# Attention on one Trainium2 core: the meta columns of two query tiles turned in one transpose

## Chip, core and metric

The kernel runs on one core of one Trainium2 chip. The metric is device time in microseconds (us) of one execution, from several executions of the same program. All matrices are float32; matmul operands are kept as a high part (rounded to the matmul's format) and a low part (the rest), so that one product becomes two or three matmuls.

## What is computed

A trunk of two layers on 2048 tokens of width 1024, with 16 learned meta tokens in front. Layer 0 is latent attention with 16 heads; layer 1 is a gated short convolution. Only the attention is touched here. Cut from the reference:

```python
key_chunk = concatenate([zeros(N_META), frame_chunk])      # N_META = 16, chunks of 64 tokens
def attend(qn, qr, q_chunk):
    s = (einsum('bqhd,bkhd->bhqk', qn, k_nope) + einsum('bqhr,bkr->bhqk', qr, k_rope)) * scale
    s = where(key_chunk[None, :] <= q_chunk[:, None], s, NEG_INF)
    p = softmax(s, axis=-1)
    return einsum('bhqk,bkhd->bqhd', p, v)
```

Every query sees the 16 meta keys and all keys up to the end of its own chunk of 64.

## The kernel before

The program has three stages, one after the other. `stage_p` makes keys, queries, values and gates (0 to 559 us of the trace). `stage_b` is the attention (to about 1564 us). `stage_cde` is the output product, the norms and the convolution layer.

**Units, tiles, chunks.** In `stage_b` each of 16 heads has 8 units (L825). A unit u is a pair of query tiles of 128 tokens, the even tile 2u and the odd tile 2u+1; unit 0 has also the tile of the 16 meta queries (`META_TILE`). The keys of a unit are cut into chunks x of 2 to 4 blocks of 128 keys; chunk 0 has the block of the 16 meta keys in front (`blocks_of`, L844). The even tile doesn't see the unit's last block (`tile_blocks`, L850).

**The steps.** Each engine works through a list of steps, written out by hand as a string of letters for one head (L829 to L840) and repeated for all heads, with lags (L841) that let scores run ahead of transposes (9 steps) and transposes ahead of products (6).
- S, TensorE (L1181 to L1191): the scores of one tile and chunk, three matmuls into one of 5 PSUM banks (`split_matmul`, L43 to L45).
- M, VectorE (L1251 to L1273): masks the last 64 keys of the diagonal block (memset, L1265) and takes the row maximum (L1267, L1272).
- E, ScalarE (L1145 to L1161): the exponential, from PSUM to one of 14 slots `p` of 512 columns in SBUF, and the row sums.
- T, TensorE (L1192 to L1209): turns the tile's chunk, one transpose for each block of keys, into `tb` (two buffers in PSUM). The data are the weights and the identity is what moves. The meta block is a transpose with 16 columns of weights. T number n waits for the exponential (L1202) and for the L step n-2 (L1204).
- H, ScalarE (L1162 to L1172): the high part of what was turned, from PSUM to `b_pt_hi`, all blocks of the chunk in one instruction.
- L, VectorE (L1274 to L1282): the low part, PSUM minus high part, to `b_pt_lo`.
- P, TensorE (L1210 to L1230): values times turned probabilities of both tiles of a unit, one matmul for each block over 256 columns (the last block of a unit has 128, the meta block of unit 0 has 272), first with the high part (L1224), then with the low part (L1228), added up in one bank `ob`. The weights are `b_v`, 128 rows by 128 columns (high and low part of the head's values); the meta block's weights have 16 rows of values, and rows of zeros under them (L1089).
- C and A: ScalarE and VectorE (L1288) take the unit's result out of `ob`.

**Beside them.** GpSimd (POOL, L1098 to L1139) splits the next head's keys, queries and values, and pieces of the output weights, into high and low parts, and multiplies earlier heads' results with their gates. SP issues all loads and stores of the stage. The identity has an SBUF tensor of its own (L2207), is loaded once near the end of `stage_p` (L345) and is used by the transposes of `stage_b` (L1207) and of `stage_cde` (L1856).

Of the kernel before, what the change touches and what calls it, by code (L numbers as in the profile page):

```python
# [6 lines left out]
F32 = mybir.dt.float32  # L7
# [6 lines left out]
P = 128  # L14
# [778 lines left out]
def own_memory(nc, ctx, outer, ident, ground, big_hi, big_lo):  # L793
# [8 lines left out]
    o_b, o_t = (arena[:, at:at + 2 * P + META] for at in (T + (NT + 1) * VH, T + (NT + 1) * VH + 2 * P + META))  # L802
    p = arena[:, sum(sizes) - PSLOTS * HALF:].rearrange("p (a b) -> p a b", b=HALF)
# [52 lines left out]

def unit_tiles(u):
    return ([META_TILE] if u == 0 else []) + [2 * u, 2 * u + 1]
# [22 lines left out]
LAST_TURNED = [max(k for k, (_, gg) in enumerate(TURNED) if gg == g) for g in range(len(PRODUCTS))]  # L881
UNIT_ENDS = [g for g, (h, u, x) in enumerate(PRODUCTS) if x == len(UNIT_CHUNKS[u]) - 1]
# [34 lines left out]
def stage_b(nc, own, dram):  # L917
# [6 lines left out]
    with ExitStack() as ctx:  # L924
        sb = lambda n, s, d=F32: ctx.enter_context(nc.sbuf_tensor(n, s, d))
        sem = lambda n: ctx.enter_context(nc.semaphore(n))
        v = sb("b_v", [P, 2, NT + 1, 2 * VH], F32R)
        pt_hi, pt_lo = sb("b_pt_hi", [P, 2, 8 * P], F32R), sb("b_pt_lo", [P, 2, 8 * P], F32R)
# [10 lines left out]
        first_hi, first_split, hi_done = sem("b_first_hi"), sem("b_first_split"), sem("b_hi_done")  # L939
        keys_loaded = lambda h: 64 * (h - 1) + 16  # L940
# [134 lines left out]
        def _(pool):  # L1075
# [66 lines left out]
        def _(act):  # L1142
            act.wait_ge(sums_set, 4)
            for letter, n in SCALAR_STEPS:
                if letter == "E":  # L1145
# [13 lines left out]
                    nc.scalar.activation(p[0:rows, n % PSLOTS, 0:w], banks[0:rows, n % RING, 0:w], ACT.Exp,  # L1159
                                         bias=nmax[0:rows, tile % 8:tile % 8 + 1],  # L1160
                                         accum_out=csum[0:rows, h % 2, j, x:x + 1]).then_inc(exps, 1)  # L1161
                elif letter == "H":  # L1162
# [5 lines left out]
                    nb, rows = len(tile_blocks(u, j, x)), tile_tokens(j)[1]  # L1168
# [3 lines left out]
                    nc.scalar.activation(turned(pt_hi, g, u, nb)[:, :, tile_columns(u, j)], tb[:, n % 2, 0:nb, 0:rows], ACT.Copy).then_inc(pt_hi_done, 1)  # L1172
# [6 lines left out]
        def _(pe):  # L1179
            for letter, n in TENSOR_STEPS:  # L1180
# [11 lines left out]
                elif letter == "T":  # L1192
# [7 lines left out]
                    _, u, j, x = SCORES[s]  # L1200
# [4 lines left out]
                    col = 0  # L1205
                    for c, (_, keys, _) in enumerate(tile_blocks(u, j, x)):
                        last = nc.tensor.transpose(tb[0:keys, n % 2, c, 0:rows], p[0:rows, s % PSLOTS, col:col + keys], ident[0:rows, 0:rows])  # L1207
                        col += keys
                    last.then_inc(t_done, 1)  # L1209
                else:  # L1210
                    h, u, x = PRODUCTS[n]
                    if n % PRODUCTS_PER_HEAD == 0:
                        if h == 0:
                            pe.wait_ge(first_split, 2)
                        else:
                            pe.wait_ge(v_split, h)
                    if x == 0 and n:
                        pe.wait_ge(o_done, h * UNITS + u)
                    blocks = blocks_of(u, x)
                    part_of = lambda c: slice(P if n in UNIT_ENDS and c == len(blocks) - 1 else 0,  # L1220
                                              2 * P + META if blocks[c][1] == META and u == 0 else 2 * P)
                    pe.wait_ge(pt_hi_done, LAST_TURNED[n] + 1)
                    for c, (k0, keys, vb) in enumerate(blocks):
                        nc.tensor.matmul(ob[:, part_of(c)], v[:, h % 2, vb, :], turned(pt_hi, n, u, len(blocks))[:, c, part_of(c)],  # L1224
                                         start=(x == 0 and c == 0), stop=False)
                    pe.wait_ge(pt_split, LAST_TURNED[n] + 1)
                    for c, (k0, keys, vb) in enumerate(blocks):
                        last = nc.tensor.matmul(ob[:, part_of(c)], v[:, h % 2, vb, :], turned(pt_lo, n, u, len(blocks))[:, c, part_of(c)],  # L1228
                                                start=False, stop=(n in UNIT_ENDS and c == len(blocks) - 1))
# [3 lines left out]
        def _(dve):  # L1233
# [15 lines left out]

            for letter, n in VECTOR_STEPS:  # L1250
                if letter == "M":  # L1251
                    if n == RING:
                        nc.vector.memset(tb[:, :, :, :], 0.0).then_inc(tb_set, 1)
                    if n == RING + 3:
                        dve.wait_ge(first_hi, 2)
                        nc.vector.tensor_tensor(v[:, 0, 1:, VH:], raw_v_blocks[:, 1:], v[:, 0, 1:, 0:VH].bitcast(F32), ALU.subtract).then_inc(first_split, 1)
                        nc.vector.tensor_tensor(v[0:META, 0, 0, VH:], raw_v_blocks[0:META, 0], v[0:META, 0, 0, 0:VH].bitcast(F32), ALU.subtract).then_inc(first_split, 1)
                    h, u, j, x = SCORES[n]
# [15 lines left out]
                elif letter == "L":  # L1274
                    if n == len(TURNED) - SUMS_BEFORE:
# [3 lines left out]
                    nb, rows = len(tile_blocks(u, j, x)), tile_tokens(j)[1]  # L1279
                    hi, lo = (turned(pt, g, u, nb)[:, :, tile_columns(u, j)] for pt in (pt_hi, pt_lo))  # L1280
# [125 lines left out]
def stage_cde(nc, ident, ground, big, o_out, r_out, gate_out, meta, meta_in, dram):  # L1406

    x_rows, og_d, o_d, z_d, r_d, ln, h_d, h_t_d, w_conv, taps_d, s_d, g_d, w_out, ln_e, out = dram
    wo_hi, wo_lo = (big[:, n * KD * D:(n + 1) * KD * D].rearrange("p (k c) -> p k c", c=D) for n in range(2))
    with ExitStack() as ctx:  # L1410
# [8 lines left out]
        ht_all, gb_all, stats = sb("c_ht", [P, 2 * KD * P]), sb("c_ln", [P, 2 * D]), sb("c_stats", [P, 2, 24])  # L1419
        cu, taps = sb("d_cu", [P, 2 * WD]), sb("d_taps", [P, 3 * KD])  # L1420
# [35 lines left out]
        ln_in = sem("c_ln_in")  # L1456
# [51 lines left out]
        def _(sp):  # L1508
# [59 lines left out]
            load(2)  # L1568
            sp.dma_start(gb_ln, ln.to_broadcast([P, 2, D])).then_inc(ln_in, 16)
# [251 lines left out]
        def _(pe):  # L1821
# [25 lines left out]
            def turn(i):  # L1847
                n = tokens(i)[1]
                pe.wait_ge(affined, i + 1)
# [382 lines left out]
```

## Time and profile before

| | us |
|---|---|
| median of three runs | 2605.08 (2601.02 to 2607.72) |
| the profiled execution, its own time | 2612.59 |
| its span, first to last instruction | 2610.8 |
| TensorE busy, matmuls (PE) | 2554.8, 98% |
| VectorE busy (DVE) | 1887.8, 72% |
| ScalarE busy (ACT) | 1442.5, 55% |
| GpSimd busy (POOL) | 429.4, 16% |
| TensorE's granted clock | 0.995 of full speed |

PE is TensorE's matmuls, PEld its weight loads, which overlap the matmuls. Matmuls are pipelined: the duration of one holds its way through the array, so what one costs is read from the start of one to the start of the next. A timeline row gives start, us from the first start to the last end, the engine, the line, what is written and read, the shape (rows x columns of the weights, then the moving part), and how many instructions were merged into the row. A row of a stretch gives its ends and length, then the busy us (and instructions) of PE, PEld, DVE, ACT and POOL, the granted clock, the DMA share and GB/s. A row of a group gives its count, busy us, mean ns of one, and the idle us ahead of them with what ended it.

### The profile page before, as it was taken

To read this page: it belongs to the slowest core of one execution; us is meant where nothing else is said; L and a number is where in the kernel's file an instruction comes from. 1 tells how busy PE (TensorE), PEld (TensorE's weight loads), DVE (VectorE), ACT (ScalarE), POOL (GpSimd) and SP (SyncE) were. 2 spreads that over 40 slices of the span, in tenths; PEclk is the share of its full clock that TensorE was granted. 3 is DMA by queue.
4 is the path that set the end of the run, shared out by engine and by line. 5 is a ranking of instruction groups with operands and counts; after the bars stand their busy time and mean duration, and the time that the engine had idled before them with its cause. 6 is when DMAs were issued, how large, how long until landed. Compare 5 with 4: busy or idle time off the path is not lost. (4 is left out here: it accounts for less than half of the span.)

```text
span 2610.8 us, 48054 instructions
## 1 busy us (share of the span) xinstructions
PE 2554.8 (98%) x17333; PEld 2403.7 (92%) x17333; DVE 1887.8 (72%) x3886; ACT 1442.5 (55%) x3529; POOL 429.4 (16%) x203
## 2 busy tenths in 40 slices
PE   8999999999999999999999999998999999999998
PEld 7999999989999999999999987888999999999787
DVE  6546651149898889898889986688877666666766
ACT  4434332248888888888888871125445445444210
POOL 0000000013344545444444400000000000000000
PEclk9999999999999999999999999999999999999999
DMA  6555454312243343333333316755544543553443
GB/s 207 188 170 183 145 157 128 94 52 45 52 100 82 83 83 83 88 82 75 87 75 82 75 44 199 225 171 195 202 178 156 201 152 130 185 188 135 143 145 112
DMA packets 245937, 337.85 MB, mean 129 GB/s; under 512 B 86338, under 2 KB 182482, under 8 KB 233234
## 3 DMA queue, kind: packets, MB, share of 16 engines
q1 hardware_dynamic: 227874, 326.40, 42.3%
q10 hardware_dynamic: 17840, 8.52, 1.1%
q8 instruction: 135, 2.21, 0.4%
q14 instruction: 88, 0.72, 0.1%
HBM read 225.34 MB, written 109.51 MB: 128 GB/s over the span
## 5 line engine op out<-in xcount | busy, mean ns | idle before, releaser
L1282 DVE TENSOR_TENSOR b_pt_lo<-b_transposed,b_pt_hi 128x384 fp32r<-128x384 f32 (+4 forms) x784 | 428.9, 564 | 50.8 <-ACT b_pt_hi L1172 47.4
L1267 DVE TENSOR_REDUCE ground<-b_ring 128x1 f32<-128x384 f32 (+7 forms) x784 | 409.0, 527 | 61.2 <-PE b_ring L45 47.8
L1172 ACT ACTIVATE b_pt_hi<-b_transposed 128x384 fp32r<-128x384 f32 (+4 forms) x784 | 382.2, 501 | 121.4 <-PE b_transposed L1207 110.1
L1159 ACT ACTIVATE ground<-b_ring,ground 128x384 f32<-128x384 f32 (+7 forms) x784 | 435.7, 560 | 19.4 <-DVE ground L1272 11.5
L1207 PE MATMUL b_transposed<-identity,ground 128*128 128x128 f32 (+2 forms) x2448 | 380.4, 272 | 10.2 <-DVE b_pt_lo L1282 6.4
L1207 PEld LDWEIGHTS b_transposed<-identity,ground 128*128 128x128 f32 (+2 forms) x2448 | 280.1, 134 | 58.4 <-issue 28.4
L43 PE MATMUL b_ring<-region 128*128 128x384 f32 (+7 forms) x784 | 300.5, 383 | 4.5 <-ACT ground L1159 3.2
L43 PE MATMUL p_banks<-p_x_hi,big 128*128 128x258 f32 x896 | 254.9, 285 | 11.2 <-DVE big L591 8.4
L45 PE MATMUL b_ring<-region 128*128 128x384 f32 (+7 forms) x784 | 257.9, 329 | 0.0
L44 PE MATMUL b_ring<-region 128*128 128x384 f32 (+7 forms) x784 | 257.6, 329 | 0.0
L45 PE MATMUL p_banks<-p_x_hi,big 128*128 128x258 f32 x896 | 254.9, 285 | 0.0
L44 PE MATMUL p_banks<-p_x_lo,big 128*128 128x258 f32 x896 | 254.4, 284 | 0.0
L1224 PE MATMUL b_o_ps<-b_pt_hi,b_v 128*128 128x256 f32 (+2 forms) x1280 | 227.7, 292 | 0.0
L405 ACT ACTIVATE ground<-p_banks 128x258 f32<-128x258 f32 (+2 forms) x194 | 80.6, 422 | 250.0 <-PE p_banks L45 223.8
L1228 PE MATMUL b_o_ps<-b_pt_lo,b_v 128*128 128x256 f32 (+2 forms) x1280 | 214.4, 282 | 0.0
L1224 PEld LDWEIGHTS b_o_ps<-b_pt_hi,b_v 128*128 128x128 f32 x1280 | 183.1, 190 | 2.9 <-DVE ground L1288 0.4
L43 PEld LDWEIGHTS p_banks<-p_x_hi,big 128*128 128x128 f32 x896 | 170.8, 191 | 11.9 <-issue 8.6
L1228 PEld LDWEIGHTS b_o_ps<-b_pt_lo,b_v 128*128 128x128 f32 x1280 | 178.8, 190 | 0.2 <-DVE b_pt_lo L1282 0.2
L44 PEld LDWEIGHTS p_banks<-p_x_lo,big 128*128 128x128 f32 x896 | 171.1, 191 | 0.4
L45 PEld LDWEIGHTS p_banks<-p_x_hi,big 128*128 128x128 f32 x896 | 170.6, 190 | 0.0
L52 POOL TENSOR_TENSOR region<-ground 64x2064 fp32r<-64x2064 f32 (+1 forms) x30 | 108.7, 3624 | 369.6 <-DMA ground<-sin_queries 186.0
L585 DVE TENSOR_TENSOR p_x_lo<-ground,p_x_hi 128x2064 fp32r<-128x2064 f32 x23 | 53.1, 2307 | 157.2 <-ACT p_x_hi L372 157.1
(215 smaller groups left out, 6382.8 us busy)
## 6 DMA issues: line engine op xcount, KB each, us to landing
ground<-x_a SPq DMA_DIRECT2D x23, 1032.0 KB, 6.0
ground<-w_conv SPq DMA_DIRECT2D x32, 512.0 KB, 3.8
c_tiles<-w_conv SPq DMA_DIRECT2D x32, 512.0 KB, 3.8
c_ln<-weight_sums SPq DMA_DIRECT2D x16, 1024.0 KB, 7.4
c_tiles<-weight_sums SPq DMA_DIRECT2D x16, 1024.0 KB, 7.1
weight_sums<-c_tiles SPq DMA_DIRECT2D x9, 1024.0 KB, 3.9
keys<-ground SPq DMA_DIRECT2D x64, 129.0 KB, 5.7
queries<-ground SPq DMA_DIRECT2D x64, 129.0 KB, 2.9
```

What stands on the lines that cost most here:

```text
L43: nc.tensor.matmul(out, w_hi, x_hi, start=start, stop=False)
L44: nc.tensor.matmul(out, w_hi, x_lo, start=False, stop=False)
L45: return nc.tensor.matmul(out, w_lo, x_hi, start=False, stop=stop)
L52: return nc.gpsimd.tensor_tensor(out, x, none.to_broadcast(shape), ALU.add)
L405: nc.scalar.activation(stage_of(r, rows), bank_of(r, rows), ACT.Silu if OUTS[r][2] == "z" else ACT.Copy, scale=SCALE if OUTS[r][2] == "q" ...
L1159: nc.scalar.activation(p[0:rows, n % PSLOTS, 0:w], banks[0:rows, n % RING, 0:w], ACT.Exp, bias=nmax[0:rows, tile % 8:tile % 8 + 1], accum_ ...
L1172: nc.scalar.activation(turned(pt_hi, g, u, nb)[:, :, tile_columns(u, j)], tb[:, n % 2, 0:nb, 0:rows], ACT.Copy).then_inc(pt_hi_done, 1)
L1207: last = nc.tensor.transpose(tb[0:keys, n % 2, c, 0:rows], p[0:rows, s % PSLOTS, col:col + keys], ident[0:rows, 0:rows])
L1224: nc.tensor.matmul(ob[:, part_of(c)], v[:, h % 2, vb, :], turned(pt_hi, n, u, len(blocks))[:, c, part_of(c)], start=(x == 0 and c == 0), s ...
L1228: last = nc.tensor.matmul(ob[:, part_of(c)], v[:, h % 2, vb, :], turned(pt_lo, n, u, len(blocks))[:, c, part_of(c)], start=False, stop=(n ...
L1267: ins = nc.vector.tensor_reduce(top, bank[0:rows, 0:w], AX, ALU.max, negate=(chunks == 1))
L1282: nc.vector.tensor_tensor(lo, tb[:, n % 2, 0:nb, 0:rows], hi.bitcast(F32), ALU.subtract).then_inc(pt_split, 1)
```

## The change

The exponential of the odd tile's chunk 0 is written 32 columns further right in its slot. VectorE copies the first 32 columns of the even tile's slot (16 meta columns and 16 that nobody uses) into the gap, one copy for each head and unit, placed in VectorE's order before the L step that is three before the odd tile's. The even tile's chunk 0 is turned without its meta block. The odd tile's meta transpose turns 48 columns: rows 0 to 15 of the result are the even tile's meta block, rows 32 to 47 the odd tile's. H and L of the even tile's chunk 0 have one block less. The meta product becomes two of 128 columns on the same turned block: with `v[..., 0, :]` (values in rows 0 to 15) for the even tile's columns, and with a new tensor `v_again` (the same values in rows 32 to 47, zeros elsewhere) for the odd tile's; unit 0 has a third one for the meta tile's 16 columns. The first product is now that of block 1, then come the meta ones. VectorE copies the values into `v_again` once a head, and GpSimd fills it with zeros at the start. For the room, the identity moves into a part of `ground` and is loaded a second time, into a tensor of `stage_cde`. The diff, cut:

```diff
-    ident = ctx.enter_context(nc.sbuf_tensor("identity", [P, P], F32))
+    ident = arena[:, T + (NT + 1) * VH + 2 * (2 * P + META):][:, 0:P]
...
+def turned_blocks(u, j, x):
+    blocks = tile_blocks(u, j, x)
+    return blocks[1:] if x == 0 and j != META_TILE and j % 2 == 0 else blocks
...
+META_COPIED = 32
+COPIES = [(SCORE_AT[h, u, 2 * u, 0], SCORE_AT[h, u, 2 * u + 1, 0]) for h in range(HEADS) for u in range(UNITS)]
+COPIES_AT = {max(TURNED_AT[odd] - 3, 0): n for n, (even, odd) in enumerate(COPIES)}
+REPEATED_AT = {TURNED_AT[SCORE_AT[h, 0, 1, 0]]: h for h in range(1, HEADS)}
+LAST_META = [PRODUCTS.index((h, UNITS - 1, 0)) for h in range(HEADS)]
+COPY_OF = {even: n for n, (even, odd) in enumerate(COPIES)}
+def tile_first(j, x):
+    return META_COPIED if x == 0 and j != META_TILE and j % 2 else 0
...
+        v_again = sb("b_v_again", [P, 2 * VH], F32R)
+        v_repeated, meta_copied = sem("b_v_repeated"), sem("b_meta_copied")
+        def turned_tile(pt, g, u, j, x):
+            first = len(tile_blocks(u, j, x)) - len(turned_blocks(u, j, x))
+            return turned(pt, g, u, len(tile_blocks(u, j, x)))[:, first:, tile_columns(u, j)]
...
+            nc.gpsimd.tensor_tensor(v_again[:, :], none, none, ALU.add).then_inc(sums_set, 1)
...
+                    if n - PSLOTS in COPY_OF:
+                        act.wait_ge(meta_copied, COPY_OF[n - PSLOTS] + 1)
+                    at = tile_first(j, x)
+                    nc.scalar.activation(p[0:rows, n % PSLOTS, at:at + w], banks[0:rows, n % RING, 0:w], ACT.Exp,
...
+                    nc.scalar.activation(turned_tile(pt_hi, g, u, j, x), tb[:, n % 2, 0:nb, 0:rows], ACT.Copy).then_inc(pt_hi_done, 1)
...
+                    for c, (_, keys, vb) in enumerate(blocks):
+                        if vb == 0 and j != META_TILE:
+                            pe.wait_ge(meta_copied, UNITS * h + u + 1)
+                            last = nc.tensor.transpose(tb[0:META_COPIED + META, n % 2, c, 0:rows], p[:, s % PSLOTS, 0:META_COPIED + META], ident[:, :])
...
+                        pe.wait_ge(v_repeated, h + 1)
...
+                    order = ([1, 0] + list(range(2, len(blocks)))) if meta else range(len(blocks))
+                    def products(pt, high):
+                        for c in order:
+                            vb = blocks[c][2]
+                            if vb:
+                                part = slice(P if n in UNIT_ENDS and c == len(blocks) - 1 else 0, 2 * P)
+                                last = nc.tensor.matmul(ob[:, part], v[:, h % 2, vb, :], turned(pt, n, u, len(blocks))[:, c, part],
+                                                        start=(high and x == 0 and c == 1), stop=(not high and n in UNIT_ENDS and c == len(blocks) - 1))
+                                continue
+                            for i, values in enumerate((v[:, h % 2, 0, :], v_again[:, :])):
+                                nc.tensor.matmul(ob[:, P * i:P * i + P], values, turned(pt, n, u, len(blocks))[:, 0, P:2 * P], start=False, stop=False)
+                            if u == 0:
+                                cols = tile_columns(u, META_TILE)
+                                nc.tensor.matmul(ob[:, cols], v[:, h % 2, 0, :], turned(pt, n, u, len(blocks))[:, 0, cols], start=False, stop=False)
+                        return last
...
+            def repeat_values(h):
+                dve.wait_ge(v_split, h)
+                dve.wait_ge(pv_done, LAST_META[h - 1] + 1)
+                nc.vector.tensor_copy(v_again[META_COPIED:META_COPIED + META, :], v[0:META, h % 2, 0, :].bitcast(F32)).then_inc(v_repeated, 1)
+            def copy_meta(k):
+                even, odd = COPIES[k]
+                dve.wait_ge(exps, even + 1)
...
+                if odd >= PSLOTS:
+                    dve.wait_ge(t_done, TURNED_AT[odd - PSLOTS] + 1)
+                nc.vector.tensor_copy(p[:, odd % PSLOTS, 0:META_COPIED], p[:, even % PSLOTS, 0:META_COPIED]).then_inc(meta_copied, 1)
...
                 elif letter == "L":
+                    if n in REPEATED_AT:
+                        repeat_values(REPEATED_AT[n])
+                    if n in COPIES_AT:
+                        copy_meta(COPIES_AT[n])
...
             load(2)
+            sp.dma_start(ident[:, :], ident_d).then_inc(ident_in, 16)
             sp.dma_start(gb_ln, ln.to_broadcast([P, 2, D])).then_inc(ln_in, 16)
```

## Rows read from the trace of the kernel before

**Rows 1.** Busy time of each engine, attention stage, then two halves of a head

```profile
566.00:1561.00 995.00, 982.86 (x7315) 921.11 (x7315) 888.87 (x2209) 847.16 (x2465) 427.69 (x192) 1.00 0.33 75
...
1056.00:1090.00 34.00, 33.92 (x254) 31.75 (x253) 31.75 (x88) 30.43 (x94) 15.12 (x6) 1.00 0.31 73
1090.00:1118.00 28.00, 27.32 (x206) 25.73 (x204) 24.10 (x51) 22.38 (x60) 15.75 (x8) 1.00 0.47 102
```

**Rows 2.** Waits of the attention stage: us in total, times, longest us

```profile
ACT b_pt_hi L1172 <- PE b_transposed L1207: 109.8, 220, 1.4
...
DVE b_pt_lo L1282 <- ACT b_pt_hi L1172: 46.5, 70, 1.1
```

**Rows 3.** Timeline of PE, a score matmul, three transposes, the next scores

```profile
1068.40 0.33 PE L45 MATMUL b_ring<-region 128*128 128x384 f32 x1
1068.81 0.49 PE L1207 MATMUL b_transposed<-identity,ground 128*16 128x128 f32 x3
1069.05 0.36 PE L43 MATMUL b_ring<-region 128*128 128x256 f32 x1
```

**Rows 4.** Timeline of PE, five transposes, two passes of products, the next transposes

```profile
1106.39 0.71 PE L1207 MATMUL b_transposed<-identity,ground 128*128 128x128 f32 x5
1106.86 0.61 PE L1224 MATMUL b_o_ps<-b_pt_hi,b_v 128*128 128x256 f32 x3
1107.30 0.51 PE L1228 MATMUL b_o_ps<-b_pt_lo,b_v 128*128 128x256 f32 x3
1108.01 0.38 PE L1207 MATMUL b_transposed<-identity,ground 128*16 128x128 f32 x2 [0.20 <-DVE b_pt_lo L1282]
```

**Rows 5.** Timeline of PE, scores of 128 columns and products of 256

```profile
1060.57 0.27 PE L45 MATMUL b_ring<-region 128*128 128x128 f32 x1
1060.68 0.34 PE L43 MATMUL b_ring<-region 128*128 128x272 f32 x1
...
1061.11 0.52 PE L1224 MATMUL b_o_ps<-b_pt_hi,b_v 128*128 128x256 f32 x3
1061.46 0.52 PE L1228 MATMUL b_o_ps<-b_pt_lo,b_v 128*128 128x256 f32 x3
```

**Rows 6.** Groups of DVE instructions by form, attention stage, then the first stage

```profile
L1282 DVE TENSOR_TENSOR b_pt_lo<-b_transposed,b_pt_hi 128x384 fp32r<-128x384 f32 x431 | 230.2, 549 | 9.7 <-ACT b_pt_hi L1172 7.5
...
L1282 DVE TENSOR_TENSOR b_pt_lo<-b_transposed,b_pt_hi 128x512 fp32r<-128x512 f32 x239 | 159.8, 685 | 39.1 <-ACT b_pt_hi L1172 39.1
...
L1265 DVE MEMSET b_ring<- 64x64 f32 x252 | 28.2, 112 | 6.8 <-PE b_ring L45 3.5
...
L1282 DVE TENSOR_TENSOR b_pt_lo<-b_transposed,b_pt_hi 128x16 fp32r<-128x16 f32 x16 | 2.6, 164 | 0.0
...
L585 DVE TENSOR_TENSOR p_x_lo<-ground,p_x_hi 128x2064 fp32r<-128x2064 f32 x23 | 53.1, 2307 | 157.2 <-ACT p_x_hi L372 157.1
...
L715 DVE TENSOR_SCALAR ground<-ground 128x2064 f32<-128x2064 f32 x1 | 1.2, 1227 | 0.0
```

**Rows 7.** Timelines of POOL and DVE at two places of head 8

```profile
1064.44 2.41 POOL L1125 TENSOR_TENSOR big<-ground,big 128x1024 fp32r<-128x1024 f32 x1
1065.11 0.26 DVE L1248 RECIPROCAL ground<-ground 128x17 f32<-128x17 f32 x1
...
1077.46 3.62 POOL L52 TENSOR_TENSOR region<-ground 64x2064 fp32r<-64x2064 f32 x1 [7.87 <-issue]
1080.87 0.41 DVE L1282 TENSOR_TENSOR b_pt_lo<-b_transposed,b_pt_hi 128x256 fp32r<-128x256 f32 x1
1081.16 4.61 POOL L1103 TENSOR_TENSOR region<-ground,region 64x2064 fp32r<-64x2064 f32 x1
```

**Rows 8.** Groups of POOL instructions by form, attention stage (two of four long ones)

```profile
L1109 POOL TENSOR_TENSOR region<-ground,region 128x2064 fp32r<-128x2064 f32 x15 | 69.6, 4640 | 1.2
...
L52 POOL TENSOR_TENSOR region<-ground 64x2064 fp32r<-64x2064 f32 x15 | 54.3, 3621 | 183.6 <-issue 178.1 <-DVE b_v L1257 5.5
```

**Rows 9.** Timeline of SP's queue, start of the third stage

```profile
1571.48 0.43 SPq L1569 DMA_DIRECT2D c_ln<-ln  x1
```

More of the change, by code:

```diff
@@ L1142, in _ @@
         def _(act):
[L1143 removed]
+            act.wait_ge(sums_set, 5)
             for letter, n in SCALAR_STEPS:
@@ L1204, in _ @@
                         pe.wait_ge(pt_split, n - 1)
-                    col = 0
-                    for c, (_, keys, _) in enumerate(tile_blocks(u, j, x)):
-                        last = nc.tensor.transpose(tb[0:keys, n % 2, c, 0:rows], p[0:rows, s % PSLOTS, col:col + keys], ident[0:rows, 0:rows])
+                    blocks = turned_blocks(u, j, x)
+                    col = META * (len(tile_blocks(u, j, x)) - len(blocks)) + tile_first(j, x)
+                    for c, (_, keys, vb) in enumerate(blocks):
+                        if vb == 0 and j != META_TILE:
+                            pe.wait_ge(meta_copied, UNITS * h + u + 1)
+                            last = nc.tensor.transpose(tb[0:META_COPIED + META, n % 2, c, 0:rows], p[:, s % PSLOTS, 0:META_COPIED + META], ident[:, :])
+                        else:
+                            last = nc.tensor.transpose(tb[0:keys, n % 2, c, 0:rows], p[0:rows, s % PSLOTS, col:col + keys], ident[0:rows, 0:rows])
                         col += keys
@@ L1222, in _ @@
                     pe.wait_ge(pt_hi_done, LAST_TURNED[n] + 1)
-                    for c, (k0, keys, vb) in enumerate(blocks):
-                        nc.tensor.matmul(ob[:, part_of(c)], v[:, h % 2, vb, :], turned(pt_hi, n, u, len(blocks))[:, c, part_of(c)],
-                                         start=(x == 0 and c == 0), stop=False)
+                    products(pt_hi, True)
                     pe.wait_ge(pt_split, LAST_TURNED[n] + 1)
-                    for c, (k0, keys, vb) in enumerate(blocks):
-                        last = nc.tensor.matmul(ob[:, part_of(c)], v[:, h % 2, vb, :], turned(pt_lo, n, u, len(blocks))[:, c, part_of(c)],
-                                                start=False, stop=(n in UNIT_ENDS and c == len(blocks) - 1))
+                    last = products(pt_lo, False)
@@ L1278, in _ @@
                     _, u, j, x = SCORES[s]
-                    nb, rows = len(tile_blocks(u, j, x)), tile_tokens(j)[1]
-                    hi, lo = (turned(pt, g, u, nb)[:, :, tile_columns(u, j)] for pt in (pt_hi, pt_lo))
+                    nb, rows = len(turned_blocks(u, j, x)), tile_tokens(j)[1]
+                    hi, lo = (turned_tile(pt, g, u, j, x) for pt in (pt_hi, pt_lo))
                     dve.wait_ge(pt_hi_done, n + 1)
@@ L2212, in program @@
             with ExitStack() as inner:
[L2213 removed]
+                own = own_memory(nc, inner, ctx, ground, big_hi, big_lo)
                 stage_p(nc, own, [ins[n] for n in ("x_a", "w_x", "w_uk", "w_uv", "w_uq", "pos", "constants", "ident")] + [k_d, kr_d, v_d, queries, z_d, sines_d])
                 stage_b(nc, own, [k_d, v_d, queries, z_d, ins["w_o"], o_d, r_d, og_d])
[L2216 to L2217 removed]
+            stage_cde(nc, ground, big, own.o_out, own.r_out, own.gate_out, own.meta, own.meta_in,
+                     [ins["ident"], ins["x_rows"], og_d, o_d, z_d, r_d, ins["ln"][0], h_d, h_t_d, ins["w_conv"], ins["taps"], s_d, g_d, ins["w_out"], ins["ln"][1], out])
 def kernel(**inputs):
```

28 lines of the change are left out of this document (15 added, 13 removed).

## Prediction

> **What bounds the kernel now.** I read the page's busy table and the stretches first. TensorE (PE) is busy 98% of the span, and in the attention stage, the only stage whose inner loops change, from 566 to 1561 us, 983 of 995 us; VectorE (DVE) 889, ScalarE (ACT) 847, GpSimd (POOL) 428 [rows 1]. A busy PE is not proof, so I read the waits next: ACT stands 109.8 us for PE's transposes, DVE 46.5 us for ACT's high parts, and no wait of PE is among the long ones [rows 2]. So PE sets the pace, with DVE close behind. One head takes 62 us and has two halves. From 1056 to 1090 DVE is busy 31.75 of 34 us and PE stands for it in places: the transposes at 1068.81 start 0.41 us after the score matmul at 1068.40, where some 0.17 is that matmul's step. From 1090 to 1118 DVE is busy 24.1 of 28 us and PE is the bound, but for one stand of 0.36 us: the last product group, 0.35 us long, starts at 1107.30, and the next transposes at 1108.01 [rows 1, 3, 4].
>
> The threshold for "no change" is 0.3%, 7.8 us, about what a measurement of this kernel can tell. The profiled execution took 2612.6 us (span 2610.8), 7.5 above the median of 2605.1; my sum is a difference worked out on its trace, set on the median.
>
> **TensorE, removed.** 128 transposes of 16 columns (8 units, 16 heads, even tile). They still stream 128 columns of the identity. From the start of a group of three transposes, one of them of 16 columns, to the next matmul it is 0.24 us; from five of full width 0.47 [rows 3, 4]. Two more transposes are 0.23, so each is worth 0.11 us, and the narrow one is no cheaper. 128 x 0.11 = 14.1 us off.
>
> **TensorE, added.** Each meta product of 256 columns becomes two of 128 with other weights, in both passes (high and low part), 256 times; unit 0 gets a third one (16 columns), 32 times. Three products of 256 columns take 0.35 us (1061.11 to 1061.46), 0.117 each. Score matmuls of 128 columns step by 0.11 us (1060.57 to 1060.68), so half the columns save almost nothing: the load of 128 weights fills the step [rows 5]. So 256 x (2 x 0.11 - 0.117) = 26.4 us, and 32 x 0.11 = 3.5 us: 29.9 on. Net PE: +15.8 us, 0.99 us a head. Here the Trainium skill speaks both ways. TensorE: Matmul & The Clock Gate, section LDWEIGHTS, says that the load goes by the weight's columns and not by its rows, 107 ns for 128, which agrees with the 0.11. The same page's gap of N/2.4 + 2.5 ns would make the two halves cost 112 ns against 109, and the sum -10 us; that is the third rival.
>
> How much of the 15.8 reaches the end? In the PE-bound half (units 4 to 6) all of 3 x (0.206 - 0.11) = 0.29 us (0.206 is 26.4 / 128). In the other half (units 7, 0 to 3) 5 x 0.096 + 0.22 = 0.70 us, of which PE's stands (the 0.24 above, and smaller ones) take in some; I let 0.3 through. 0.59 x 16 = +9.4 us; bounds 4.6 (none of the second half) and 15.8.
>
> **VectorE and ScalarE.** The low part of the even tile's first chunk loses one block of 128 columns: 685 to 549 ns is 0.136, and a block less is worth the same at the other widths; 128 x 0.136 = 17.4 us off DVE. ACT loses a block too, at most as much, which only lengthens its waits for PE. The 128 copies of 32 columns cost each between the memset of 112 ns and the 16-column subtraction of 164 ns: +14 to +21 us; 16 copies of the values at most +2.6 [rows 6]. DVE comes out level, -3 to +6 us, and I take nothing for it. The copy's own waits are over when it comes: the schedule runs the scores nine steps ahead of the transposes, so that the even tile's exponential is long done, and PE's new wait is on a copy that stands ahead of a subtraction (three turns back) for whose successor the transpose waits anyway. The value copy's waits, on the last head's unit 7 and on the split, are met a unit before.
>
> **Beside GpSimd.** The copy is the first DVE instruction of this stage that reads and writes SBUF alone with one source, at a double rate: in the first stage, with POOL idle, such a form takes 1227 ns for 2064 columns, against 2307 ns with two sources [rows 6]. Two columns a cycle need a second way into the memory, and POOL, whose instructions here are of 1.3 to 4.6 us, is the other engine that works in SBUF all through this stage. No row shows such a form beside POOL. The lower bound is nothing: the reciprocal at 1065.11 ran beside POOL's subtraction (1064.44 to 1066.85) in 0.26 us [rows 7]. But at 0.26 us for 17 columns it is far from a double rate, so it doesn't speak for the copy. The upper bound is that a copy waits until POOL's running instruction has ended. Placed at random, a copy waits the sum of count x duration^2 / 2 over 995 us: the long instructions, two groups of 15 at 4.63 us and two at 3.62, give 1036 / 2 / 995 = 0.52 us, 67 us for 128 copies, and the shorter ones of 0.3 to 2.4 us bring it to 87 [rows 8]. Placed at the 128 starts of the subtractions before which they will stand, 43 (first in head 0, last in head 15) meet a POOL instruction and wait 42 us in all, mostly in units 3 and 6. In unit 3 of head 8 the subtraction at 1080.87 finds POOL's 3.62 us from 1077.46 nearly over, 0.2 us to wait; but POOL's next, of 4.61 us, starts at 1081.16, and a DVE that is 0.3 us later meets that one whole [rows 7]. So I take 42 to 87 and, with some of those slips, 55 us, nine tenths of it on the path, since DVE has next to no slack in half of each head; in exchange PE's own extra work hides behind DVE's stands: 50 + 5 left = +50 to +55 us; I take 50. The Trainium skill (SBUF — State Buffer, Who interferes with whom) says that a copy in a two-port mode and a GpSimd instruction exclude each other for the whole of the one that came first; by it the sum would be this upper one, and no run here shows it yet.
>
> **The edges.** The identity is loaded again in the next stage: one more issue on SP, of some 0.43 us, ahead of the norm's load at 1571.48, whose rows the first norm needs before PE needs the identity [rows 9]. On SP it delays the loads behind it by 0.4 us; where the stage waits for them that is the cost, 0 to 0.4 us. POOL fills one more tile before ACT starts, while ACT loads its table. The identity's new place is loaded at the same point as before. I take nothing for all.
>
> **Forecast and rivals.**
> Forecast (0.55): copies wait for POOL, 2605 + 50 = 2655 us, own range 2625 to 2700. For it: the double rate, and POOL busy 43% of the stage. Against it: no row has shown the wait.
> Rival 1 (0.24): the copies cost 0.11 to 0.16 us and wait for nobody; PE's weight loads decide: +9.4, 2614 us (2610 to 2621). For it: all PE rows. It decides where POOL leaves the copies alone.
> Rival 2 (0.11): as rival 1, but DVE's half takes in all of PE's extra and ACT's shorter work closes the chain: +4, 2609 us, no change. For it: PE's stands. Against it: they are short and at few places.
> Rival 3 (0.06), faster: a product of half the columns costs half, so only the transposes count, with 3.5 us at most for the third product: -10 to -14 us, 2594 us. It decides if the step falls below 0.06 us. Against it: the score matmuls of 128 columns at 0.11.
> Rival 4 (0.04): the slips put most copies of unit 3 into POOL's long instruction: 15 x 4 us on top, over 2700.
>
> The range reaches from just above rival 2's middle to the forecast's upper part: 2610 to 2693 us. Faster by over 0.3%: 0.07 (rival 3 and a remainder). Within 0.3%: 0.15 (rival 2, the low end of rival 1). Slower: 0.78.
>
> **What would show it.** In the profile after: copies on DVE of about 0.15 us where POOL is idle, and of 1 to 4 us, or with idle time ahead of them, where it is busy; DVE's busy time in the stage up by tens of us; PE standing longer for DVE, most in units 3 and 6. Transposes 128 fewer; three products per pass where two stood, each at a step of 0.11. If all copies last 0.15 us and the stage grows by about 10 us, rival 1 was right; if the half products step by 0.06, rival 3. A change outside the attention stage of over 2 us would be something I haven't seen.

## The result, and the profile after

Four runs of the changed kernel have a median of 2664.09 us (2649.44 to 2671.58), four of the kernel before on the same chip 2606.07 (2601.02 to 2607.72). The ratio is 1.0221, 95% interval 1.0201 to 1.0241: 58 us slower. The forecast was 2655 in a range of 2610 to 2693, and its likeliest case is the one that came. The changed kernel also varies more, 22 us against 7. Its profiled execution took 2671.58 us (span 2669.8) and is the longest of the four.

First the page of the changed kernel: its busy table, the lines' part of the chain that ended last (cut to the line that has it), and two groups (busy us, mean ns | idle before and its releaser):

```profile
PE 2580.0 (97%) x17493; PEld 2433.5 (91%) x17493; DVE 1936.1 (73%) x4030; ACT 1432.2 (54%) x3529; POOL 429.1 (16%) x204
...
PE b_o_ps L1264 9%; PE b_transposed L1242 8%; PE cd_banks L1470 7%; PE cd_banks L1471 7%; PE cd_banks L1472 7%; PE b_ring L43 5%; PE b_ring L45 5%; PE b_ring L44 5%; PE cd_banks L44 5%; PE cd_banks L43 5%; PE cd_banks L45 5%; DVE ground L1311 2%; PE b_o_ps L1268 2%; DVE ground L1332 1%; DVE b_pt_lo L1351 1%
...
L1202 ACT ACTIVATE b_pt_hi<-b_transposed 128x384 fp32r<-128x384 f32 (+4 forms) x784 | 372.0, 484 | 185.6 <-PE b_transposed L1242 167.7
...
L1242 PE MATMUL b_transposed<-ground 128*128 128x128 f32 (+1 forms) x2192 | 355.7, 274 | 45.5 <-DVE b_pt_lo L1351 41.5
```

PE is still busy 97%, yet the copies' line, L1311, holds 2% of the chain, 42 us. PE's share of the page hardly moved while a wait of 41.5 us for DVE appeared in front of its transposes. The stretch that [rows 1] show of before, and the waits that answer to [rows 2] (us in total, times, longest), of the changed kernel:

```profile
566.00:1561.00 995.00, 948.67 (x7040) 894.66 (x7040) 882.46 (x2218) 786.31 (x2323) 419.14 (x188) 0.99 0.32 73
```

```profile
ACT b_pt_hi L1202 <- PE b_transposed L1242: 158.1, 228, 3.7
...
PE b_transposed L1242 <- DVE b_pt_lo L1351: 39.6, 25, 3.6
DVE b_pt_lo L1351 <- ACT b_pt_hi L1202: 38.4, 66, 1.1
```

In the same 995 us PE is busy 34 us less than before and does 275 matmuls fewer. ACT waits 48 us longer for PE, and PE waits 39.6 us for DVE in only 25 places, the longest 3.6 us: a few long stops, not a tax on each head.

The forms of DVE's instructions in the changed kernel's attention stage, with the copies (L1311) and the low parts (L1351, L1282 of before in [rows 6]), then the value copies (L1301); in a second view the line of the copies by itself (ns, shortest/median/longest, first and last start):

```profile
L1351 DVE TENSOR_TENSOR b_pt_lo<-b_transposed,b_pt_hi 128x384 fp32r<-128x384 f32 x480 | 258.3, 549 | 40.8 <-ACT b_pt_hi L1202 38.1
...
L1351 DVE TENSOR_TENSOR b_pt_lo<-b_transposed,b_pt_hi 128x512 fp32r<-128x512 f32 x160 | 108.3, 685 | 8.4 <-ACT b_pt_hi L1202 5.3
...
L1311 DVE COPY ground<-ground 128x32 f32<-128x32 f32 x128 | 65.7, 514 | 0.5 <-issue 0.5
...
L1301 DVE CAST b_v_again<-b_v 16x128 fp32r<-16x128 f32 x15 | 3.3, 217 | 0.7 <-PE b_o_ps L1264 0.3
```

```profile
L1311 DVE COPY ground<-ground x128: 168/181/4272, 565.5 to 1610.9; 128x32 f32<-128x32 f32 x128
```

The median copy takes 0.18 us and the mean one 0.51. Here is the difference, at one place of head 7 of the changed kernel, the timeline of all engines cut to the rows that matter:

```profile
1065.76 3.63 POOL L52 TENSOR_TENSOR region<-ground 128x2064 fp32r<-128x2064 f32 x1 [9.76 <-DMA ground<-sin_queries]
1065.86 0.16 DVE L1337 TENSOR_REDUCE ground<-ground 128x1 f32<-128x4 f32 x1
1065.94 3.48 DVE L1311 COPY ground<-ground 128x32 f32<-128x32 f32 x1
...
1069.34 1.14 DVE L1351 TENSOR_TENSOR b_pt_lo<-b_transposed,b_pt_hi 128x384 fp32r<-128x384 f32 x2
...
1070.03 0.52 PE L1242 MATMUL b_transposed<-ground 128*128 128x128 f32 x3 [2.96 <-DVE b_pt_lo L1351]
```

POOL's splitting of the queries starts at 1065.76 and ends at 1069.39. The copy starts 0.18 us behind it and ends at 1069.42. The subtraction that waits in line behind it starts at 1069.34, and PE has stood 2.96 us for it. The copy shows no idle time in front of it: the wait is inside its duration, and so DVE looks busy. The chain of the same place passes through it:

```profile
1065.86 0.04 DVE ground L1337
...
1065.94 3.48 DVE ground L1311
1069.42 0.47 DVE b_pt_lo L1351
...
1070.03 0.52 PE b_transposed L1242 x3
```

Of the 128 copies, 87 start with POOL idle and take 168 to 184 ns, 15.2 us together. The other 41 start inside a POOL instruction and take 50.5 us together; 38 of them end 35 to 47 ns after it. With 0.174 us as a copy's own time the waits are 65.7 - 128 x 0.174 = 43.4 us. 16.9 us of them stand in unit 5, where in five heads the copy takes 3.3 to 3.8 us; 14.7 in unit 6 (copies of 0.5 to 2.3 us in most heads); 5.4 in units 0 and 1 of head 0; 3.5 in unit 3 (0.2 to 0.7 us).

By the profiled executions the attention stage, from its first score matmul to its last product, went from 1003.7 to 1066.9 us.

**TensorE's clock.** A stop of PE cost more than itself in places. Three stretches follow: in head 7 of the changed kernel, behind the stop above, that of a low clock, then that of the 15 matmuls that start in it, and last that of the same 15 in experiment 2 below, whose TensorE work is the same:

```profile
1070.49:1073.90 3.41, 3.41 (x17) 3.25 (x16) 2.19 (x4) 1.76 (x4) 3.41 (x1) 0.50 0.02 5
1070.61:1074.09 3.48, 3.48 (x17) 3.28 (x16) 2.07 (x4) 1.88 (x5) 3.44 (x1) 0.53 0.02 5
```

```profile
1035.94:1037.90 1.96, 1.96 (x16) 1.85 (x16) 1.50 (x4) 1.81 (x7) 1.96 (x1) 1.00 0.03 8
```

After PE had stood for 2.96 us its granted clock fell to half, 1.2 GHz, and work of 1.96 us took 3.48. The changed kernel's attention stage has eight such stretches, 27 us in all. Seven of them lie beside a stop of PE of 2.4 to 3.6 us for a copy, and the eighth is at the start of the stage; two stops of 2.3 and 2.4 us have none beside them. In its attention stage the kernel before has one such stretch, experiments 1 and 2 have none. Laid matmul by matmul beside experiment 2's trace, the eight together cost 11.5 us.

The first stage ended 3.3 us earlier than before, though nothing in its loops was changed. About 1.5 us of this is the clock too. The kernel before, then the changed one:

```profile
22.20:25.60 3.40, 3.40 (x18) 3.40 (x18) 2.60 (x3) 3.15 (x3) 0.00 (x0) 0.50 0.89 302
```

```profile
22.20:25.60 3.40, 3.40 (x28) 3.29 (x27) 2.66 (x4) 2.12 (x3) 0.00 (x0) 1.00 0.97 388
```

Five of the thirteen profiles have this low stretch near 22 us, and in them the stage ends at 557.9 to 561.5 us; in the eight without it, at 555.0 to 556.5. What else differs in the first 100 us was not found.

### The profile page after: what moved, and what is told of

Read it like the earlier page. It is cut to its first block, busy times and chain, and to the rows that moved or that the text cites. A ratio compares the mean times of both kernels' runs of the same rounds, so it can differ in the third digit from the quotient of the medians.

```text
span 2669.8 us, 48775 instructions
## 1 busy us (share of the span) xinstructions
PE 2580.0 (97%) x17493; PEld 2433.5 (91%) x17493; DVE 1936.1 (73%) x4030; ACT 1432.2 (54%) x3529; POOL 429.1 (16%) x204
## 4 chain that ended last, share of the span: by engine, by line
PE 69%; DVE 6%; ACT 1%; DMA 1%; issue 1%; SPq 0%; POOL 0%; DVEq 0%; ACTq 0%; POOLq 0%
PE b_o_ps L1264 9%; PE b_transposed L1242 8%; PE cd_banks L1470 7%; PE cd_banks L1471 7%; PE cd_banks L1472 7%; PE b_ring L43 5%; PE b_ring L45 5%; PE b_ring L44 5%; PE cd_banks L44 5%; PE cd_banks L43 5%; PE cd_banks L45 5%; DVE ground L1311 2%; PE b_o_ps L1268 2%; DVE ground L1332 1%; DVE b_pt_lo L1351 1%
## 5 line engine op out<-in xcount | busy, mean ns | idle before, releaser
L1202 ACT ACTIVATE b_pt_hi<-b_transposed 128x384 fp32r<-128x384 f32 (+4 forms) x784 | 372.0, 484 | 185.6 <-PE b_transposed L1242 167.7
L1351 DVE TENSOR_TENSOR b_pt_lo<-b_transposed,b_pt_hi 128x384 fp32r<-128x384 f32 (+4 forms) x784 | 412.7, 542 | 49.5 <-ACT b_pt_hi L1202 43.4
L1242 PE MATMUL b_transposed<-ground 128*128 128x128 f32 (+1 forms) x2192 | 355.7, 274 | 45.5 <-DVE b_pt_lo L1351 41.5
L1242 PEld LDWEIGHTS b_transposed<-ground 128*128 128x128 f32 (+1 forms) x2192 | 264.8, 140 | 81.7 <-issue 42.3
L1264 PE MATMUL b_o_ps<-b_pt_hi,b_v 128*128 128x256 f32 (+1 forms) x1152 | 243.0, 302 | 0.1
L1264 PE MATMUL b_o_ps<-b_pt_lo,b_v 128*128 128x256 f32 (+1 forms) x1152 | 227.9, 289 | 0.0
L1264 PEld LDWEIGHTS b_o_ps<-b_pt_lo,b_v 128*128 128x128 f32 x1152 | 173.4, 191 | 0.2 <-DVE b_pt_lo L1351 0.2
```

Source lines behind the costliest of these rows:

```text
L1202: nc.scalar.activation(turned_tile(pt_hi, g, u, j, x), tb[:, n % 2, 0:nb, 0:rows], ACT.Copy).then_inc(pt_hi_done, 1)
L1264: last = nc.tensor.matmul(ob[:, part], v[:, h % 2, vb, :], turned(pt, n, u, len(blocks))[:, c, part], start=(high and x == 0 and c == 1), ...
L1351: nc.vector.tensor_tensor(lo, tb[:, n % 2, 0:nb, 0:rows], hi.bitcast(F32), ALU.subtract).then_inc(pt_split, 1)
```

## The experiments

Theory: a DVE copy inside SBUF is held until POOL's running instruction has ended, and this is most of the 58 us; the rest is PE's net work. Rivals: any additional step at that place of DVE's order costs this; or the cost is PE's (the split products), and the long copies only fill time that DVE had. "Before" is always the kernel before, run beside the kernel on the same chip. Stage lengths are of the profiled execution.

**1. The copies on ScalarE** (all else as changed):

```diff
+                nc.scalar.activation(p[:, odd % PSLOTS, 0:META_COPIED], p[:, even % PSLOTS, 0:META_COPIED], ACT.Copy).then_inc(meta_copied, 1)
-                nc.vector.tensor_copy(p[:, odd % PSLOTS, 0:META_COPIED], p[:, even % PSLOTS, 0:META_COPIED]).then_inc(meta_copied, 1)
```

> The changed kernel, with the 128 copies moved from VectorE to ScalarE (before the H step of the same number). Theory A (the copies wait for GpSimd's running instruction; the wait is VectorE's alone): no copy lasts longer than about 0.25 us beside GpSimd, and what is left is TensorE's extra work of 9 to 16 us: 2615 to 2625 us. Rival (the time comes from TensorE's additional weight loads and the products' order, and the long copies only fill VectorE's free time): 2645 us or more.

Measured: 2616.42 us (5 runs), ratio 1.0041 (1.0027 to 1.0056), +10.6 us; the stage takes 1012.7. Repeated later as it was, with this expectation:

> e1 once more, on the same chip as e9, so that the two can be compared: 2612 to 2620 us by either theory.

it gave 2616.78 (6 runs), ratio 1.0042 (1.0029 to 1.0054). 48 of the 58 us go with the copies' engine. ScalarE's copies, by duration:

```profile
L1178 ACT ACTIVATE ground<-ground x128: 214/228/255, 564.3 to 1554.5; 128x32 f32<-128x32 f32 x128
```

None waits, wherever POOL is.

**2. The same copies on VectorE, at the same place, as another instruction**: a maximum over an axis of length one.

```diff
-                nc.vector.tensor_copy(p[:, odd % PSLOTS, 0:META_COPIED], p[:, even % PSLOTS, 0:META_COPIED]).then_inc(meta_copied, 1)
+                nc.vector.tensor_reduce(p[:, odd % PSLOTS, 0:META_COPIED], p[:, even % PSLOTS, 0:META_COPIED].rearrange("p (a b) -> p a b", b=1), AX, ALU.max).then_inc(meta_copied, 1)
```

> The changed kernel, with each copy done by VectorE as a maximum over an axis of one element: same place, same data, one source, but an instruction that moves one column a cycle. Theory A (only the double-rate form needs what GpSimd holds): each lasts 0.15 to 0.2 us also beside GpSimd, 2617 to 2630 us. Rival 1 (every VectorE instruction that reads and writes SBUF alone waits for GpSimd): as long as the copies, 2650 to 2670 us.

Measured: 2621.07 (4 runs), ratio 1.0054 (1.0037 to 1.007); stage 1017.9. All instructions of the line, and one of them in the timeline, head 0's in unit 5, with 3.82 us of a POOL instruction of 4.64 still to run. Then the same place of the changed kernel:

```profile
L1311 DVE TENSOR_REDUCE ground<-ground x128: 174/182/188, 565.4 to 1561.9; 128x32 f32<-128x32 f32 x128
```

```profile
591.77 4.64 POOL L1136 TENSOR_TENSOR region<-ground,region 128x2064 fp32r<-128x2064 f32 x1
...
592.59 0.19 DVE L1311 TENSOR_REDUCE ground<-ground 128x32 f32<-128x32 f32 x1
...
592.69 1.15 DVE L1351 TENSOR_TENSOR b_pt_lo<-b_transposed,b_pt_hi 128x384 fp32r<-128x384 f32 x2
```

```profile
598.23 4.56 POOL L1136 TENSOR_TENSOR region<-ground,region 128x2064 fp32r<-128x2064 f32 x1
...
599.04 3.79 DVE L1311 COPY ground<-ground 128x32 f32<-128x32 f32 x1
```

41 of the 128 start inside a POOL instruction here too, and the longest takes 0.188 us, where the copy took 3.79. So neither the place in the order nor one more DVE step is what costs: 43 us lie between two instructions that move the same 32 columns. This is the run that decides between the theory and its first rival.

**3. Copies alone, nothing else of the change**: before, with 128 copies into columns of the slots that nobody reads.

```diff
+                nc.vector.tensor_copy(p[:, odd % PSLOTS, 480:512], p[:, even % PSLOTS, 0:32]).then_inc(meta_copied, 1)
```

> The kernel before, with 128 copies of 32 columns in the same place of VectorE's order and with the same waits, into columns of the slot that nobody reads: TensorE's work is unchanged. Theory A: some 40 of the copies wait for GpSimd, 35 to 55 us in all, and as no subtraction gets shorter VectorE has 128 x 0.17 = 22 us more besides: 2645 to 2680 us. Rival (the copies hide in VectorE's 100 us of free time): 2606 to 2615 us.

Measured: 2642.91 (4 runs, 2634.48 to 2648.80), ratio 1.0145 (1.0127 to 1.0164), +37 us: two us under what was expected. Its profiled execution was its shortest; there the waits are 42.1 - 128 x 0.17 = 20 us, and the stage is 29.2 longer than before's. In what is left are the copies' own time and the low clock, which lasts for 20 us of the stage against 3 of before's.

**4. The split products alone**: before, with the meta product in two (three in unit 0), on the same weights.

```diff
+                    parts_of = lambda c: [part_of(c)] if blocks[c][2] else [slice(0, P), slice(P, 2 * P)] + ([tile_columns(u, META_TILE)] if u == 0 else [])
+                    for c in order:
+                        for part in parts_of(c):
+                            last = nc.tensor.matmul(ob[:, part], v[:, h % 2, blocks[c][2], :], turned(pt_hi, n, u, len(blocks))[:, c, part],
```

> The kernel before, with only the meta product split: two products of 128 columns (and a third of 16 in unit 0) with the same weights, block 1 first; no copy, all transposes. Theory A (a product of 128 columns takes a step of 0.11 us): 29.9 us more on TensorE, of which its waits for VectorE take in some: 2624 to 2636 us. Rival (half the columns cost half): 2606 to 2611 us.

Measured: 2627.78 (4 runs), ratio 1.0082 (1.0062 to 1.0102), and again later, with

> e4 once more, on the same chip as e9: 2624 to 2632 us by either theory.

2626.49 (4 runs), ratio 1.0079 (1.0057 to 1.0101): +21 to +22 us. Here the timeline can mislead. One pass of products of the changed kernel:

```profile
1063.76 0.28 PE L1264 MATMUL b_o_ps<-b_pt_lo,b_v 128*128 128x256 f32 x1
1063.88 0.22 PE L1268 MATMUL b_o_ps<-b_pt_lo,b_v 128*128 128x128 f32 x1
1063.94 0.28 PE L1268 MATMUL b_o_ps<-b_pt_lo,b_v_again 128*128 128x128 f32 x1
1064.06 0.45 PE L1264 MATMUL b_o_ps<-b_pt_lo,b_v 128*128 128x256 f32 x2
...
1064.35 0.34 PE L43 MATMUL b_ring<-region 128*128 128x384 f32 x1
```

The second half starts 0.06 us after the first, as if a half product cost half (rival 3). But the two that follow take 0.29, where two take 0.24 elsewhere: the step that the halves saved is paid behind them. From 1063.76 to 1064.35 five products take 0.59 us. In experiment 4's trace all 80 low-part passes of this form have a median of 0.581 us, against 0.479 for the 96 passes of four whole products in before's: 0.102 a split product, where the forecast had 0.103. The third product of unit 0, of 16 columns only, adds 0.098 more (0.569 against 0.369 for the two together). Cost is to be read over the group, not from one step.

**5. The even tiles' meta transposes taken out, nothing added**: they, and one block of the H and L steps, are left out, and with them the meta keys' share in the even tiles.

```diff
-                    for c, (_, keys, _) in enumerate(tile_blocks(u, j, x)):
+                    for c, (_, keys, _) in enumerate(turned_blocks(u, j, x)):
```

> The kernel before without the even tile's meta transposes; ScalarE's and VectorE's high and low parts of that chunk have one block less, the products are as before and read what stands in the meta block's even columns, so the meta keys' share of the even tiles is left out; GpSimd fills the two buffers once at the start. Theory A (each transpose is worth a step of 0.11 us, 14.1 us in all, less where VectorE sets the pace, and VectorE has 17 us less to do): 2590 to 2599 us. Rival (a narrow transpose costs little): 2603 us or more.

Measured: 2607.16 (10 runs, 2600.76 to 2613.87) against 2604.15 of before in 13, ratio 1.0007 (0.9992 to 1.0023). It missed: in the median nothing came of 14.1 us of PE work. The stage is 4.1 us shorter in the profiled execution, 3.1 of it in one head where the kernel before happened to have a stop and a low clock. But a head that runs undisturbed is 0.5 us shorter, 61.3 against 61.8, 8 us over 16 heads. The waits suggest where a part of the rest went (attention stage of experiment 5, then of before):

```profile
DVE ground L1307 <- ACT ground L1193: 23.2, 65, 3.9
ACT ground L1174 <- DVE ground L1289: 20.7, 91, 1.8
```

```profile
ACT ground L1159 <- DVE ground L1272: 11.5, 42, 1.5
DVE ground L1288 <- ACT ground L1176: 8.4, 35, 0.6
```

The exponential now waits for the maximum 9 us longer, and the unit's result on DVE 15 us longer for ScalarE. PE was given time, and the chain between ACT and DVE may have taken a part of it; no run shows that by itself. Another part is the experiment's own: ScalarE's first exponential stands 1.82 us for GpSimd, which fills the buffers first, PE stands 2.33 us for it, and a clock of 0.50 follows from 564.7 to 571.5 us. After the first head this kernel is 1.5 us behind before's.

**6. The copy as an addition of zeros**, two sources in SBUF:

```diff
+                nc.vector.tensor_tensor(p[:, odd % PSLOTS, 0:META_COPIED], p[:, even % PSLOTS, 0:META_COPIED], zero[:, 0:1].to_broadcast([P, META_COPIED]), ALU.add).then_inc(meta_copied, 1)
```

> The changed kernel, with each copy done by VectorE as an addition of a column of zeros: both sources and the result in SBUF, one column a cycle. Theory A in its wider form (GpSimd holds the second way into SBUF, which a second source needs as much as a double rate): some 40 of them wait for GpSimd, 2648 to 2672 us. Theory A in its narrow form (only the double rate waits): 0.15 to 0.2 us each, 2617 to 2626 us, as the maximum over one element.

Measured: 2654.44 (4 runs, 2644.56 to 2660.76), ratio 1.0186 (1.0157 to 1.0215); stage 1053.8. The same picture as the copy's, at 0.19 us or up to the end of POOL's instruction:

```profile
L1311 DVE TENSOR_TENSOR ground<-ground x128: 179/191/4268, 565.6 to 1597.7; 128x32 f32<-128x32 f32 x128
```

```profile
1057.31 3.63 POOL L52 TENSOR_TENSOR region<-ground 128x2064 fp32r<-128x2064 f32 x1 [9.85 <-DMA ground<-sin_queries]
...
1057.40 3.58 DVE L1311 TENSOR_TENSOR ground<-ground 128x32 f32<-128x32 f32 x1
```

So it isn't the copy's double rate alone: an addition that reads two SBUF sources is held as well.

**7. POOL's long instructions cut in four** (keys' and queries' splits, 3.6 and 4.6 us), the copies as changed:

```diff
-                nc.gpsimd.tensor_tensor(q_lo[:, h % 2, :], raw[:, :], q_hi[:, h % 2, :].bitcast(F32), ALU.subtract).then_inc(q_split, 1)
+                for at in QUARTERS:
+                    lo = nc.gpsimd.tensor_tensor(q_lo[:, h % 2, at], raw[:, at], q_hi[:, h % 2, at].bitcast(F32), ALU.subtract)
```

> The changed kernel, with GpSimd's four long instructions a head (rounding and subtraction of keys and of queries, 3.6 and 4.6 us) each cut in four of a quarter of the columns. Theory A (a copy waits to the end of the running instruction, so the longest wait is that of the longest instruction): no copy beside those waits longer than about 1.3 us, the sum of the waits falls from some 44 to 15 to 30 us, and the time to 2625 to 2650 us. Rival (it is the share of time in which GpSimd is busy that counts, not how long one instruction is): 2655 to 2672 us.

Measured: 2643.78 (4 runs), ratio 1.0164 (1.0147 to 1.0181); stage 1036.5, waits 39.4 - 22.3 = 17.1 us.

```profile
L1319 DVE COPY ground<-ground x128: 170/181/1776, 564.6 to 1579.7; 128x32 f32<-128x32 f32 x128
```

No copy takes more than 1.03 us beside the quarters; the longest, 1.78, stands beside an instruction of 1.9 us for the values, which were not cut. Shorter foreign instructions make shorter waits.

**8. The changed kernel once more**, one execution, to see whether the same program with other waits takes another time:

> The changed kernel once more, for a second profile. Theory A: the time follows the sum of the copies' waits in that execution: with 43.6 us of waits the profiled one took 2671.6; each us of waits less takes about 1 us off. Rival: the time differs from 2671.6 by several us with the same sum of waits.

Measured: 2648.74 us; copies 50.4 us in all, waits 28.1; stage 1047.4. That is 23 us less than the first profiled execution with 15 us less of waits: 8 us more than one for one, in direction as expected. The stage alone is 19.5 shorter, of which 5.5 come from the clock, which was low for 17 us of it and not for 27; 3.4 us lie outside the stage.

**9. The split products without the even transposes, no copies** (it leaves out the same share as 5), to see what the transposes are worth where PE has more to do:

> The kernel before with both of TensorE's edits and no copy: the meta product split as in e4, the even tile's meta transposes left out as in e5 (so again the meta keys' share of the even tiles is left out). Theory (the removed transposes are worth nothing alone because VectorE and the irregular heads set the time there, but nearly their 14 us once the split makes TensorE the bound; ScalarE's copies in e1 cost next to nothing): 2612 to 2618 us, as e1. Rival (the removed transposes are worth nothing anywhere, and e1 gains by something else, the moved tiles or the wider gap): 2624 to 2630 us, as e4.

Measured: 2621.39 (4 runs), ratio 1.0059 (1.0041 to 1.0076). Beside experiment 11's 2626.49 on the same chip, the transposes are worth 5 us of 14.1, between the two expectations. But this kernel has experiment 5's fills as well: PE stands 2.31 us near the start, the clock is at 0.50 from 559.7 to 563.1, and after the first head it is 1.5 us behind experiment 11's. The heads away from it are clearer. Of heads 1, 3, 5, 7, 9, 11 and 13 (counted from 0), which are the least disturbed, the median length in us (from a head's first scores to the next one's):

| kernel | head | less before's |
|---|---|---|
| before | 61.78 | |
| 5, no even transposes | 61.29 | -0.49 |
| 4 and 11, products split | 63.24 and 63.22 | +1.45 |
| 9, both | 62.63 | +0.85 |
| 1 and 10, all of the change, copies on ScalarE | 62.57 and 62.57 | +0.79 |
| 2, the same, copies as maxima on VectorE | 62.83 | +1.05 |

So a head's removed transposes are worth 0.60 us beside the split and 0.49 alone, of 0.88 counted, and experiments 1 and 9 agree within 0.06: ScalarE's copies cost nothing. That bears out the theory beside the split, and not its "nothing alone".

With experiment 2 as the kernel without waits (stage 1017.9), the four executions with waits line up. The fourth column is by how much the same matmuls fell further behind experiment 2's in the stretches of low clock:

| profiled execution | waits of the copies | stage longer than experiment 2's | of it by the low clock | the rest, for each us of waits |
|---|---|---|---|---|
| changed | 43.4 | 49.0 | 11.5 | 0.86 |
| 6 | 32.0 | 35.9 | 8.2 | 0.87 |
| 8 (changed again) | 28.1 | 29.5 | 6.0 | 0.84 |
| 7 | 17.1 | 18.6 | 1.4 | 1.01 |

## Why the prediction was right, and where its terms were off

**The main case.** It said that a copy waits for POOL's running instruction; 41 of 128 did (43 had been placed), and experiments 1, 2 and 7 show it from three sides. The Trainium skill (SBUF — State Buffer, Who interferes with whom) says that a copy in a two-port mode and a GpSimd instruction exclude each other, that an instruction with two SBUF inputs contends with a GpSimd one that reads SBUF, and that a reduce never does on this chip. The traces agree with all three: a copy took 3.48 us and an addition 3.58 under a POOL instruction of 3.63, and a maximum 0.19 with 3.82 us of one still to run. That the placed waits of 42 us meet the 43.4 of the profile so closely is in part luck: another execution of the same kernel had 28.1.

**The sum.** By medians the 58 us fall apart into three terms, each the difference of two kernels:

| term | forecast | measured | from |
|---|---|---|---|
| PE's net work | +9.4 | +10.6 | experiment 1 less before |
| DVE's copies, no waits | 0 (-3 to +6) | +4.7 | experiment 2 less 1 |
| waits for POOL, with what the clock adds | 50 (55 x 0.9) | +43.0 | changed less experiment 2 |

The step that failed, in size, is the last one of the sum: "in exchange PE's own extra work hides behind DVE's stands: 50 + 5 left", of which 50 was taken. Little of it hides. The stops are at 25 places and PE's extra work is in every unit; without any wait it costs 10.6 us (experiment 1), and of 43.4 us of waits 37.5 reach the stage's end, so at most 6 us of anything hide behind them. The factor of nine tenths came out, at 0.84 to 1.01. What the sum left out is the low clock after the long stops, 11.5 us in the profiled execution and 6.0 in the other. Against that, the waits were put too high, 55 for 43 and 28. So the mechanism was right, and part of the closeness of 50 to 58 is errors that cancel.

**PE's term** is right for reasons that hold singly only in part. The step of 0.102 us a split product was forecast at 0.103, so 29.9 us of matmul work was right, but alone it costs 21 to 22 (1.45 us in an undisturbed head, of 1.87). That the half of a head in which DVE is the bound takes in the rest was argued in the forecast and is not shown by itself. The removed transposes were counted at 14.1 us; by the undisturbed heads they are worth 7.8 alone and 9.6 beside the split, and experiments 5 and 9 show less in their medians, in part because their own fills cost time at the start. The net is 0.79 us in an undisturbed head, where the forecast let 0.59 of 0.99 through. The Trainium skill (TensorE: Matmul & The Clock Gate, section Back-to-back issue gap) gives N/2.4 + 2.5 ns as the gap of an isolated matmul; worked out from it, as an estimate, two halves would have 112 ns against 109 for one whole. The passes above show 0.102 us more for the split, and as much for a product of 16 columns, so the columns that stream don't decide here; the load of 128 weights, which all of them share, fits.

**DVE's term.** A copy takes 0.17 us with POOL idle, just above the bound of 0.164. In the timeline the next instruction starts 0.09 us after it (1105.35 and 1105.44, head 8), so less than its duration is on DVE's path.

**Where the waits are.** In unit 3 the copies took 0.2 to 0.7 us. Rival 4, the slips of that unit into POOL's long one, didn't come; early in an instruction of 4.5 to 4.6 us only head 0's copies of units 1 and 5 fell (4.27 and 3.79 us). Unit 5 was not foreseen: in head 3 its copy started at 800.57, 0.28 us before POOL's 3.63, and took 0.18; in head 7 it started 0.18 us after and took 3.48. Between the two profiled executions of the changed kernel, 23 us apart, the waits differ by 15, 13 of them in unit 5. So this hit or miss, with the low clock behind each long stop, makes most of that difference, and by it probably most of the kernel's spread of 22 us.

**The rivals.** Rival 1 (no wait, 2614) is what experiment 1 shows, 2616: its price was right and its condition false here. Rival 2 (2609) fell with it. Rival 3 fell by the 0.102. What was to be seen came: DVE busy 48 us more by the page, 128 transposes fewer (2448 before; 2192 at L1242 and 128 of 48 columns at L1240 after), three products for two. What was not: 3.3 us outside the stage, about half of it the clock.

No version beat the kernel before. The best of the changed ones is experiment 1's, and it is 0.4% slower: the transposes that it saves cost less than what the split products add.

## What to carry over

Where GpSimd works in SBUF, keep VectorE's copies inside SBUF, and its operations on two SBUF sources, off the critical order: give them to ScalarE, or use a form that isn't held, as the maximum here. Their wait stands inside their duration, so the profile shows a busy VectorE; compare the shortest, median and longest of the line, and lay the long ones beside GpSimd's timeline. Look at the granted clock behind every long stop of PE: here it fell to half behind stops of 3 us, and each time some 1.5 us were lost on top. And a matmul cut in two cost a whole further step of 0.10 us here; the steps inside the group don't tell it, its total does.

## What had not been expected of the hardware

An instruction that changes nothing but its form was 43 us apart over 128 uses: a maximum over one element is never held (0.174 to 0.188 us), a copy is. The conversion of the values (16 rows, 128 columns, 0.217 us) is held too: in experiment 2, and in 7, one of 16 took 1.3 us, ending within 0.1 us of a POOL instruction of 1.29 us that had started just before it. And most held instructions end 35 to 47 ns after POOL's (44 to 55 for the one with two sources), although alone it takes 0.17 us: a part of its own work lies inside the wait.
